# Handing the transposed, split x1 from the second phase to the attention phase through DRAM

## What is computed

```
x1 = x + conv_mixer(x)                       # layer 0
# shared keys and values, and layer 1, both start from a normalised x1
h  = x1 * rsqrt(mean(x1*x1) + eps)           # gains are folded into the weights
k, v = split(h @ w_kv);  q, z = split(h @ w_in_b)
o  = sliding_window_attention(norm(q), norm(k), v, sinks)   # 128 wide, 16 heads, 4 key heads
y  = x1 + (o * silu(z)) @ w_out_b
```

## Time and profile before

| | |
|---|---|
| median of the runs | 2042.77 us |
| span of the profiled execution | 2040.9 us |
| TensorE busy | 1877.6 us (92%) |
| VectorE, ScalarE, GpSimd busy | 1187.5, 960.7, 554.8 us |
| granted TensorE clock, mean | 0.950 |
| DMA, mean | 82 GB/s |

### The profile page before, as it was taken

How to read it: one execution, slowest core, us unless ns; L and a number is a source line. 1 busy time by engine, 2 the same in 40 slices (tenths; PEclk the granted TensorE clock), 3 DMA queues, 4 the chain that set the end, 5 groups by cost and what they waited for, 6 DMA issues and landing times. The chain is left out here.

```text
span 2040.9 us, 29317 instructions
## 1 busy us (share of the span) xinstructions
PE 1877.6 (92%) x9991; PEld 1499.5 (73%) x9991; DVE 1187.5 (58%) x1985; ACT 960.7 (47%) x1877; POOL 554.8 (27%) x536
## 2 busy tenths in 40 slices
PE   5999999789999579999999997589999999999988
PEld 3888886568888367888888875467777777777666
DVE  3168877998888546788753333455555554555410
ACT  5366765656767353323323323445454545545410
POOL 0068984668889201221221211000000000000000
PEclk9999999889999789999999999689999999999976
DMA  5111114202111544223232213312112111211210
GB/s 177 61 47 67 42 51 138 86 31 68 53 67 48 173 160 167 92 104 117 91 109 99 82 66 115 127 64 93 49 49 87 59 49 65 82 49 60 70 46 17
DMA packets 106598, 167.18 MB, mean 82 GB/s; under 512 B 36115, under 2 KB 58619, under 8 KB 106471
## 3 DMA queue, kind: packets, MB, share of 16 engines
q1 hardware_dynamic: 106519, 166.22, 24.4%
HBM read 116.09 MB, written 52.78 MB: 83 GB/s over the span
## 5 line engine op out<-in xcount | busy, mean ns | idle before, releaser
L313 POOL TENSOR_TENSOR a_csum<-a_prod,a_csum 128x512 f32<-128x512 f32 x308 | 403.6, 1310 | 75.5 <-ACT a_prod L382 26.1
L486 DVE SCALAR_TENSOR_TENSOR a_acc<-a_vbuf,taps,a_acc 128x512 f32<-128x512 f32 x476 | 318.3, 748 | 0.0
L382 ACT ACTIVATE a_prod<-a_vbuf,taps 128x512 f32 (+1 forms) x322 | 224.4, 718 | 107.5 <-POOL a_csum L313 91.0
L109 PE MATMUL a_psg<-w,a_xt 128*128 128x512 f32 (+1 forms) x816 | 200.9, 403 | 13.1 <-DVE a_xt L457 9.2
L109 PE MATMUL a_psz<-a_w,a_xt 128*128 128x512 f32 (+1 forms) x816 | 198.5, 398 | 6.9 <-DVE a_w L97 6.9
L109 PE MATMUL c_acc<-w,c_ht 128*128 128x512 f32 (+1 forms) x816 | 201.1, 403 | 1.5 <-DVE c_sz L1455 0.7
L109 PE MATMUL c_acc<-c_w,c_ot 128*128 128x512 f32 (+1 forms) x816 | 198.1, 399 | 4.0 <-DVE c_ot L1447 2.2
L109 PE MATMUL a_psa<-w,a_xt 128*128 128x512 f32 (+1 forms) x816 | 195.7, 395 | 6.4 <-DVE w L97 6.3
L109 PE MATMUL b_pso<-w,b_yt 128*128 128x512 f32 (+1 forms) x816 | 192.2, 395 | 1.1 <-DVE b_yt L968 1.1
L109 PEld LDWEIGHTS a_psg<-w,a_xt 128*128 128x128 f32 (+1 forms) x816 | 152.2, 190 | 49.8 <-DVE a_xt L457 13.8
L109 PE MATMUL b_psq<-b_w,b_ht 128*128 128x512 f32 (+1 forms) x816 | 188.1, 389 | 0.0
(11 more groups left out here) (165 smaller groups left out, 2615.0 us busy)
## 6 DMA issues: line engine op xcount, KB each, us to landing
a_x<-in_x_prompt SPq DMA_DIRECT2D x32, 512.0 KB, 3.6
a_stage<-in_w_in_a SPq DMA_DIRECT2D x48, 256.0 KB, 2.8
z_d<-a_zo SPq DMA_DIRECT2D x32, 256.0 KB, 2.3
b_cz<-c_d SPq DMA_DIRECT2D x16, 512.0 KB, 5.2
b_cz<-z_d SPq DMA_DIRECT2D x16, 512.0 KB, 6.0
b_x<-in_x_prompt SPq DMA_DIRECT2D x16, 512.0 KB, 3.3
x_d<-b_x SPq DMA_DIRECT2D x16, 512.0 KB, 2.7
q_d<-b_qo SPq DMA_DIRECT2D x16, 512.0 KB, 2.7
```

What stands on the lines that cost most here:

```text
L109: last = pe.matmul(out, xt[:, a, k, 0:n], w[:, b, k], start=(k == 0 and a == 0 and b == 0), stop=(k == KT - 1 and b == 1))
L313: pool.tensor_tensor(csum[:, j], prod[:, i % RING], csum[:, j], ALU.add).then_inc(prod_added, 1)
L382: act.activation(prod[:, i % RING], win, ACT.Identity, scale=wcol(DTAPS + i, cs * CT + j), bias=bcol(cs * CT + j) if i == 0 and u < 2 else ...
L486: dve.scalar_tensor_tensor(csum[:, j] if k == DTAPS - 1 else acc[:, i], win, wcol(k, s * CT + j), csum[:, j] if k == 0 else acc[:, i], ALU ...
```

## The change

Phase b stores both parts of `ht` of each tile to a new DRAM tensor `ht_d` (17 x 128 rows of 8 KB). Its SP issues `store_ht(t-1)` ahead of `store_x1(t)`, and its ScalarE waits, before it overwrites `ht`, for that store to have landed (`ht_out`). Phase c loads `ht` from there and has no `hx`, `scale_h`, `turn_h` and `cut_h`. `load_ht(t+1)` waits for both z projections of tile t, as `ht` is one buffer there too, and stands on SP after `load_res(t-1)`. In the sample tile 64 of 128 columns are moved, so its DRAM pieces are 256 bytes long.

```diff
 # phase b, SP
+            def store_ht(t):
+                n = rows_of(t)
+                sp.wait_ge(hlo_ready, t + 1)
+                rows = g.ht_d[bass.ds(t * P, P)] if not isinstance(t, int) else g.ht_d[t * P:(t + 1) * P]
+                sp.dma_start(rows[:, :, :, 0:n], f32(ht[:, :, :, 0:n])).then_inc(ht_out, 16)
...
                     load_left(left)
+                if not (isinstance(t, int) and t == 0):
+                    store_ht(t - 1)
                 store_x1(t)
...
             split_weights_dma(sp, io.w_in_b[:, D + HALF:2 * D], g, 4)
+            store_ht(ALL - 1)
             store_qkv(ALL - 1)
+            sp.wait_ge(ht_out, 16 * ALL)
 # phase b, ScalarE, cut_h
                 after(act, q_mm, t)
+                after(act, ht_out, 16 * t)
                 act.activation(ht[:, 0, :, 0:n], ps_t[:, :, 0:n], ACT.Copy).then_inc(hhi_ready, 1)
 # phase c, SP
-            def load_h(t):
-                after(sp, th_done, t)
-                n = rows_of(t)
-                sp.dma_start(hx[0:n], token_rows(g.x1_d, t, n)).then_inc(hx_in, 16)
+            def load_ht(t):
+                after(sp, z_mm, 2 * t)
+                n = rows_of(t)
+                rows = g.ht_d[bass.ds(t * P, P)] if not isinstance(t, int) else g.ht_d[t * P:(t + 1) * P]
+                sp.dma_start(f32(ht[:, :, :, 0:n]), rows[:, :, :, 0:n]).then_inc(ht_in, 16)
...
-                load_h(t + 1)
                 if not first:
                     load_res(t - 1)
+                load_ht(t + 1)
                 load_q(t + 1)
 # phase c, ScalarE: scale_h and cut_h and their calls are gone
-                scale_h(t + 1)
                 split(0)
...
-                cut_h(t + 1)
                 copy_gate(t * KVH + 1, 1)
 # phase c, VectorE: cut_h and its calls are gone
-                cut_h(t + 1)
                 split(10)
 # phase c, TensorE
-                turn_h(t + 1)
                 pv(t, 1, r, loads)
...
             def turn_q(t):
                 pe.wait_ge(q_in, 16 * (t + 1))
-                pe.wait_ge(hlo_ready, t + 1)
+                after(pe, qt_ready, t)
...
             def z(t, b):
                 n = rows_of(t)
-                pe.wait_ge(hlo_ready, t + 1)
+                pe.wait_ge(ht_in, 16 * (t + 1))
 # program
+        g.ht_d = nc.dram_tensor("ht_d", (ALL * P, 2, KT, P), F32, kind=SCRATCH).ap()
```

More of the change, by code:

```diff
@@ L676, in phase_b @@
         left_in, left_step, left_out = sem("b_left_in"), sem("b_left_step"), sem("b_left_out")
+        ht_out = sem("b_ht_out")
         heads = lambda ap, m: ap.rearrange("p (h d) -> p h d", h=m)
@@ L1159, in phase_c @@
         g.wslot = g.shared_slots + [sb(f"c_w{m}", [P, 2, KT, HALF], F32R) for m in range(2, 4)]
-        hx = sb("c_hx", [P, D])
         xr = sb("c_xr", [P, D])
@@ L1197, in phase_c @@
         v_in = [sem("c_v_in0"), sem("c_v_in1")]
-        (tab_in, sinkd_in, hx_in, xr_in, q_in, y_out, bias_made, nsink_made, h_ready, th_done, hhi_ready, hlo_ready,
+        (tab_in, sinkd_in, ht_in, xr_in, q_in, y_out, bias_made, nsink_made,
          tq_done, qt_ready, tk_done, kt_ready, z_mm, ztanh_ready, zg_done, qk_done, s_read, m_ready, nm_ready,
@@ L1201, in phase_c @@
          ohi_ready, olo_ready, out_mm, res_done, szt_done, szt_ready, od_ready) = (sem("c_" + x) for x in (
-             "tab_in sinkd_in hx_in xr_in q_in y_out bias_made nsink_made h_ready th_done hhi_ready hlo_ready "
+             "tab_in sinkd_in ht_in xr_in q_in y_out bias_made nsink_made "
              "tq_done qt_ready tk_done kt_ready z_mm ztanh_ready zg_done qk_done s_read m_ready nm_ready "
@@ L1266, in store_y @@
                 sp.dma_start(io.y_s if n == DEC else token_rows(io.y_p, t, n), xr[0:n]).then_inc(y_out, 16)
-            load_h(0)
+            load_ht(0)
             load_q(0)
@@ L1313, in _ @@
         def _(act):
-            def scale_h(t):
-                n = rows_of(t)
[L1316 to L1324, removed]
             def cut_o(t):
@@ L1378, in copy_gate @@
                 act.activation(szc[:, 2 * kv:2 * kv + 2, :], ps_o[:, 2 * P:4 * P].rearrange("p (k n) -> p k n", k=2), ACT.Copy).then_inc(snt_ready, 1)
-            scale_h(0)
-            cut_h(0)
             queries(0)
@@ L1438, in _ @@
         def _(dve):
[L1439 to L1442, removed]
             def cut_o(t):
@@ L1670, in out @@
                 project(pe, acc[0:n], ot, g.wslot[OUT0 + b], n, (g.w_lo, KT * b) if gate else None).then_inc(out_mm, 1)
-            turn_h(0)
             turn_q(0)
```

## The result

| | changed kernel | kernel before, beside it |
|---|---|---|
| median of the runs (lowest to highest) | 2049.03 us (2045.26 to 2050.78, 12 runs) | 2043.41 us (2040.97 to 2045.71, 12 runs) |
| ratio | 1.0027, 95% interval 1.0019 to 1.0036 | |
| span of the profiled execution | 2047.8 us | 2040.9 us |
| granted TensorE clock, mean | 0.944 | 0.950 |

What follows compares the result with a forecast made beforehand. TensorE, busy 1877.6 of 2040.9 us, was taken to wait for ScalarE, and ScalarE for the x1 load. Terms -5.2 + 3.9 + 8.1 = +6.8 us on 2042.77 gave 2049.6 us, 0.33% slower, range 2044 to 2056.

Steps and rivals of the forecast that it cites:

- Items 1 and 2: Attention phase: removing the eight transposes of x1 (16 times) and the two float32r cuts in steady tiles gains nothing.
- Rival A: Faster: TensorE's own queue sets the start of P times V, transposes pay 0.87 us in 15 tiles; 2036.6 us, 7%.
- Item 3: Attention tiles 2 to 15: without scale_h on ScalarE ahead of the exponentials, 5.2 us gained; bounds 3 and 8.
- Items 4 and 5: Steady tiles: loading the two parts in the attention phase and storing them in the second phase cost nothing.
- Item 6: Start of second phase: ScalarE's cut of tile 1 waits for the ht store, 3.9 us lost; bounds +1 and +8.
- Item 7: End of second phase: the last ht store, in 256-byte pieces, is hidden and costs nothing; bounds 0 and +4.
- rival C: Far slower: 256-byte pieces at 40 GB/s, store lasting 13 us, plus first attention tile at its upper bound; 2060 us, 13%.
- Item 8: First attention tile: weight pieces queue on SP behind load_ht(1), which waits for z(0,1); 8.1 us lost, bounds +4 and +13.
- D: The forecast itself for the whole kernel: slower by +4.1 to +13 us; 62%.
- B: Within 0.2%: one of the two start-up waits (second phase, first attention tile) is absent or given back; 18%.

Runs made afterwards that it cites:

- e3: Changed kernel with eight transposes of the identity, result unused, where turn_h stood; 2049.82 us, ratio 1.0041 to the kernel before.
- e4: Kernel before with only the second phase's ht stores and ScalarE's wait for them, attention phase as it was; 2044.30 us, ratio 1.0014 to the kernel before.
- e7: Kernel before with its two DRAM cache copies in round 10 of phase b, not round 0; 2038.67 us, ratio 0.9986 to the kernel before.
- e5: Kernel before with the load of x1 for phase c issued a tile earlier; 2040.27 us, ratio 0.9986 to the kernel before.
- e2: Changed kernel with the store of tile 0's ht issued ahead of the two cache copies; 2048.01 us, ratio 1.0030 to the kernel before.
- e10: Changed kernel with the cache copies moved to phase c, behind the last load of tile 14; 2041.70 us, ratio 0.9998 to the kernel before.
- e9: Kernel before with the cache copies moved to phase c, behind the last load of tile 14; 2047.43 us, ratio 1.0025 to the kernel before.
- e1: Changed kernel with load_ht(1) issued behind the 14 weight pieces in the first attention tile; 2037.47 us, ratio 0.9975 to the kernel before.
- the best version: Changed kernel with load_ht(1) behind the weight pieces and the cache copies in the attention phase; 2032.20 us, ratio 0.9952 to the kernel before.
- e8: Changed kernel with load_ht(1) behind the weight pieces, store_ht(0) moved to right before the key gain's load, cache copies in mid phase b; 2034.49 us, ratio 0.9955.

## Why the prediction was right

The sign and the size were right, 2049.6 forecast and 2049.03 measured, but an agreement to 0.6 us is luck: single executions of one kernel spread over 5 us, and of the 6.9 us between the two profiled spans 2.4 lie ahead of K, where nothing was changed. Step by step it stands as follows.

**Items 1 and 2, the transposes and cuts, nothing: right.** The wait for ScalarE's copy grew by 0.87 us where 0.87 us of transposes went, and e3, which puts the transposes back, has the same rest to 0.1 us. Rival A is refuted. The cuts were taken out of phase c together with the rest and have no run of their own.

**Item 3, scale_h, -5.2 forecast: the mechanism right, and its size in this pair of profiles.** The distances from QK to z lost 5.1 us of excess. The whole stretch lost 6.1; the rest is the shorter wait for the cache's keys in the sample tile (1.5), against 0.3 more in tile 1, and neither was in the sum. The 5.2 are partly luck all the same, for they are the excess of one execution: it was 4.1 in e4 and 3.1 in e7, with the same phase c. And e5 shows that I named the work removed and should have named the load: an earlier load alone gives steady tiles as short.

**Items 4 and 5, steady loads and stores, nothing: right.** The steady rounds of phase b last what they did (30.73 to 30.76 us from QKV to QKV, 30.73 or 30.74 before), and in phase c z follows QK in tiles 2 to 15 without a wait for the load.

**Item 6, start of phase b, +3.9 forecast, +4.0 in the pair: the wait right, the size less sure.** The cut came 16.7 us after K, forecast were 16.2. But four profiles with the store at this place average 506.05 us to phase c and two without it 503.2, 2.8 us less, and e4 gives 2.0 by its medians. I had also put all of it down to the wait. e2 shows a second chain, the z load, that holds QKV at K + 24.6 us when the wait is gone, 1.4 later than in before; but e5, without any store, has z as late, so that this remainder is the store's isn't shown. Behind both chains stand the two copies (e10). The working did let the store follow them, with its landing counted from the moment SP went on, but it took their delay as given; e7 and e9 show that it cost the kernel before 3 us at QKV, and by e10 the change costs nothing here without it.

**Item 7, end of phase b, nothing: right.** The 256-byte pieces, 0.5 MB of them, were hidden in front of the q store, landed in 4.4 us where rival C needed 13. C is out.

**Item 8, first attention tile, +8.1 forecast, +6.6 measured: right, a fifth too large.** The pieces 4 and 5 were cut 39.6 us into phase c, 8.35 us later than before and not 9.5: z(0,1) ended 0.7 us sooner than I took it to, and the second of the pair wasn't the extra 1 us late. From there to the QK block it lasts 1.7 us less, 1.4 were forecast. e1 puts a number on the whole cause, one load's place in a queue: 11.3 us, which is more than the loss, since without it the other half of item 8, the work left out in the first tile, is seen as a gain of 4.7 (2.9 and 1.4 were forecast).

**The rivals.** D came. B is out: both start-up waits were there, at the places named, though by the time alone it is narrow (0.19% to 0.36%, B was within 0.2%). The sum misses by 2.3 us in the pair of profiles (+4.5 against +6.8): 1.5 are item 8, and 0.9 the last stretch, by the sample tile and not by item 3.

## What to carry to other kernels

When an engine is 99% busy, look at what ends each wait at its edge before counting the work taken off it: here 12.7 us of TensorE work were worth nothing, and one late load, ahead of an unrelated operation in ScalarE's order, held 3 to 5 us of waits in the profiles of the old order (e7, before), though the median of e5 moved by 1.0 only. When a DMA is added to or moved on an in-order issuing engine, list what it stands behind and what stands behind it, in bytes and in the semaphore it waits for, above all in the rounds that run once: the same change was 5.6 us slower with a load ahead of the weight pieces and 4.9 faster with it behind them. And try the reordering without the change too: the earlier load and the moved copies alone gave 9.0 of the 10.5 us of the best version.

## What the runs showed of the hardware

The two DRAM to DRAM copies of 960 KB cost SP 0.7 to 0.8 us each to issue (1.2 in e2, behind the new store), and then hold back what SP issues next. Behind them, in the changed kernel, a 1 MB store landed 14.6 us after its issue and the 512 KB store behind that one 15.4; without them it was 5.3 and 4.5 (e10). What that costs depends on the place: 1.8 us in a full round of phase b (e7), 4.75 in the same round with the ht store (e8), 9 us of TensorE's time in tile 15 where the next load is waited for (e9), and under 0.5 there where it is not (e10: tile 15 to the end 151.2 us, 150.9 in the changed kernel). The mean DMA share, 0.2 in phase c, tells nothing of this.

Behind the stalls of the first attention tile the clock comes back at different moments though phase c is the same program: 0.80 and 0.72 were granted in the 10 us shown for e1 and e6, a mixture of the levels of 1.2 and 2.4 GHz, and the first z projection in them took 6.53 and 7.37 us. That is 0.8 us between two profiles which no edit in phase c explains; the two kernels differ in phase b, and their first tiles by 0.6 us.
